# First mixer, two-head units: the first head's turned outputs move from a job's pair of PSUM banks to banks 6 and 7

## What is computed

```python
def ab_mixer(xn, w_in, w_out, lower_bound, a_gnorm, w_gk, b_gk, b_gnorm, s_a, s_b):
    h = jnp.einsum('btd,de->bte', xn, w_in)
    a_q, a_f, a_i, a_g, b_q, b_k, b_v, b_g, b_lr = split_cols(h, AB_SIZES)
    ...
    o_b, s_b_new = gated_linear_recurrence(
        heads(b_q * (B_DK ** -0.5), B_HEADS), heads(b_k, B_HEADS), heads(b_v, B_HEADS),
        heads(log_alpha, B_HEADS), s_b)
    o_b = rmsnorm(o_b, b_gnorm) * jax.nn.silu(heads(b_g, B_HEADS).astype(F32))
    o = jnp.concatenate([o_a.reshape(bsz, t_len, -1), o_b.reshape(bsz, t_len, -1)], axis=-1).astype(xn.dtype)
    return jnp.einsum('bte,ed->btd', o, w_out), s_a_new, s_b_new
```

## Time and profile before

| | us |
|---|---|
| median of 3 runs | 1423.03 |
| lowest, highest run | 1423.01, 1424.56 |
| the profiled execution, its own time | 1427.3 |
| its span, first to last instruction | 1425.5 |
| PE busy in the span | 1391.0 |
| DVE, ACT, POOL busy | 587.2, 558.6, 591.4 |

### The profile page before, as it was taken

How to read it: one execution, slowest core, us unless ns; L and a number is a source line. 1 busy time by engine, 2 the same in 40 slices (tenths; PEclk the granted TensorE clock), 3 DMA queues, 4 the chain that set the end, 5 groups by cost and what they waited for, 6 DMA issues and landing times.

```text
span 1425.5 us, 27289 instructions
## 1 busy us (share of the span) xinstructions
PE 1391.0 (98%) x11038; PEld 1312.6 (92%) x11038; DVE 587.2 (41%) x1068; ACT 558.6 (39%) x907; POOL 591.4 (41%) x303
## 2 busy tenths in 40 slices
PE   8999999999999999999999999999999999999997
PEld 6778898899999999999989778778999999999997
DVE  6615556464321223123425967654633113311234
ACT  5634556445332233122455344444543223321222
POOL 3332222243544344434445466554244433452442
PEclk9999999999999999999999999999999999999999
DMA  5221122242333223322232322111233323332221
GB/s 180 75 74 49 49 77 66 67 130 62 98 85 111 59 88 89 105 73 74 84 103 72 89 76 77 53 31 30 60 89 89 104 74 88 88 104 74 81 68 63
DMA packets 204486, 114.34 MB, mean 80 GB/s; under 512 B 16500, under 2 KB 198648, under 8 KB 204408
## 3 DMA queue, kind: packets, MB, share of 16 engines
q1 hardware_dynamic: 199056, 109.47, 26.4%
q10 hardware_dynamic: 5352, 3.76, 0.8%
HBM read 107.26 MB, written 5.96 MB: 79 GB/s over the span
## 4 chain that ended last, share of the span: by engine, by line
PE 71%; issue 20%; POOL 6%; DVE 1%; ACT 0%; POOLq 0%; DVEq 0%; ACTq 0%
PE ps L1149 57%; POOL w_lo L596 6%; PE ps L1337 3%; PE ps L1284 3%; PE ps L1299 1%; PE ps L1610 1%; PE ps L1654 1%; PE ps L1622 1%; PE ps L1348 0%; PE ps L1646 0%; PE ps L1585 0%; PE ps L1539 0%; DVE small L2205 0%; ACT arena L971 0%; DVE arena L2323 0%
## 5 line engine op out<-in xcount | busy, mean ns | idle before, releaser
L596 POOL TENSOR_TENSOR w_lo<-w_raw,w_hi 128x1024 fp32r<-128x1024 f32 x202 | 501.7, 2487 | 723.5 <-ACT w_hi L661 723.5
L1149 PE MATMUL ps<-x_hi,w_hi 128*128 128x272 f32 (+1 forms) x1840 | 384.7, 290 | 6.2 <-POOL w_lo L596 3.2
L1149 PE MATMUL ps<-x_hi,w_lo 128*128 128x272 f32 (+1 forms) x1840 | 381.6, 289 | 0.0
L1149 PE MATMUL ps<-x_lo,w_hi 128*128 128x272 f32 (+1 forms) x1840 | 380.3, 288 | 0.0
L1149 PEld LDWEIGHTS ps<-x_hi,w_hi 128*128 128x128 f32 (+1 forms) x1840 | 288.9, 188 | 13.5 <-issue 7.0
L1149 PEld LDWEIGHTS ps<-x_lo,w_hi 128*128 128x128 f32 (+1 forms) x1840 | 289.1, 188 | 0.5
L1149 PEld LDWEIGHTS ps<-x_hi,w_lo 128*128 128x128 f32 (+1 forms) x1840 | 287.3, 189 | 0.5
L661 ACT ACTIVATE w_hi<-w_raw 128x1024 fp32r<-128x1024 f32 x202 | 211.4, 1050 | 166.8 <-PE ps L1149 138.6
L1149 PE MATMUL ps<-o_hi,w_hi 128*128 128x272 f32 x832 | 172.4, 288 | 0.2 <-DVE xT L1854 0.2
L1149 PE MATMUL ps<-o_hi,w_lo 128*128 128x272 f32 x832 | 172.2, 288 | 0.0
L1149 PE MATMUL ps<-o_lo,w_hi 128*128 128x272 f32 x832 | 171.5, 288 | 0.0
(11 more groups left out here) (310 smaller groups left out, 1738.0 us busy)
## 6 DMA issues: line engine op xcount, KB each, us to landing
w_raw<-in_ffn_w_in SPq DMA_DIRECT2D x88, 512.0 KB, 3.7
w_raw<-in_ffn_w_out SPq DMA_DIRECT2D x32, 512.0 KB, 3.7
w_raw<-in_ab_w_in SPq DMA_DIRECT2D x28, 512.0 KB, 3.6
w_raw<-in_cd_w_in SPq DMA_DIRECT2D x13, 512.0 KB, 3.6
w_raw<-in_ffn_w_out SPq DMA_DIRECT2D x16, 384.0 KB, 3.4
w_raw<-in_ab_w_out SPq DMA_DIRECT2D x8, 512.0 KB, 4.2
arena<-in_x_prompt SPq DMA_DIRECT2D x4, 512.0 KB, 5.6
w_raw<-in_cd_w_in SPq DMA_DIRECT2D x8, 256.0 KB, 3.4
```

The lines of the kernel that those rows point to most:

```text
L596: pool.tensor_tensor(wl[:, s, :], raw[:, s, :], wh[:, s, :].bitcast(F32), ALU.subtract).then_inc(lo_done, 1)
L1149: mm = pe.matmul(ps[0:M, b + h, 0:HALF], w[:, s, k * M:(k + 1) * M], xs[x][:, k, h * HALF:(h + 1) * HALF], start=(begin and k == ks[0] and ...
```

## The change

The turn of the first head in units 0 and 1 leaves the list of pair users and writes banks 6 and 7, out of which that head's outputs have been read by then. It gets a count of its own, `turn_free`, which `head_gate(u, 0)` raises when it has read the two banks and on which `head_hi(u, 0)`, `head_lo(u, 0)` and the next unit's `turn_and_score` wait. As one entry is gone from the list, the entries behind it move up by one place: the gate job of head 1 takes place 12 (banks 0 and 1), the turn of head 1 place 13 (banks 2 and 3), the score, key and query entries of the next unit the other pair than before, and from the gate job of head 1 of unit 1 on, where two entries are gone, every entry has its old pair again.

```diff
         for e, c0 in enumerate([AG + i * P] if kind == "a" else [BG + 2 * i * P, BG + (2 * i + 1) * P]):
             unit_chunk(c_gates[u], c0)
-            order.append(("turn", u, e))
+            if kind == "a" or e:
+                order.append(("turn", u, e))
...
+        turn_free = sem("turn_free")
+        def turn_bank(u, e):
+            return 2 * (jof["turn", u, e] % 2) if ("turn", u, e) in jof else 6
+        def turn_taken(u, e):
+            return frees(("turn", u, e)) if ("turn", u, e) in jof else turn_free
+        def wait_turn_taken(eng, u, e):
+            if ("turn", u, e) in jof:
+                wait_freed(eng, ("turn", u, e))
+            else:
+                eng.wait_ge(turn_free, units[u][1] + 1)
...
             def head_hi(u, e):
-                wait_freed(act, ("turn", u, e))
+                wait_turn_taken(act, u, e)
...
             def turn_and_score(u):
                 if u > 0:
                     pe.wait_ge(r_r, (NB + 1) * u)
+                    if last(u - 1):
+                        pe.wait_ge(turn_free, units[u - 1][1] + 1)
...
             def turn_outputs(u, e):
-                j = jof["turn", u, e]
                 pe.wait_ge(r_tm, 2 * (heads_before[u] + e + 1))
-                wait_pair(j)
+                if ("turn", u, e) in jof:
+                    wait_pair(jof["turn", u, e])
...
-                    mm = pe.transpose(at(2 * (j % 2), n0, n1), ktm[0:n1 - n0, t, :], ident[0:n1 - n0, 0:n1 - n0])
+                    mm = pe.transpose(at(turn_bank(u, e), n0, n1), ktm[0:n1 - n0, t, :], ident[0:n1 - n0, 0:n1 - n0])
...
             def head_gate(u, e):
-                gn, b0 = pc("ga" if units[u][0] == "a" else "gb"), 2 * (jof[key] % 2)
+                gn, b0 = pc("ga" if units[u][0] == "a" else "gb"), turn_bank(u, e)
...
-                ins.then_inc(frees(key), 1)
+                ins.then_inc(turn_taken(u, e), 1)
...
             def head_lo(u, e):
-                wait_freed(dve, ("turn", u, e))
+                wait_turn_taken(dve, u, e)
```

More of the change, by code:

```diff
@@ L2031, in head_gate @@
             def head_gate(u, e):
-                h, key = heads_before[u] + e, ("turn", u, e)
+                h = heads_before[u] + e
                 dve.wait_ge(r_ot, h + 1)
```

## The result

The changed kernel is slower: a median of 1429.69 us (6 runs, 1426.49 to 1430.66) against 1424.02 us (6 runs, 1423.01 to 1427.25), ratio 1.0037 with a 95% interval of 1.0027 to 1.0048, which is 3.8 to 6.8 us. Taken once more beside other kernels it gave 1429.66 against 1423.66 us, ratio 1.0048 (1.0034 to 1.0062). I had forecast 1423.0 us and no change, with an upper end of 1426.2 us.

The account below looks back on a forecast made before the run. PE, busy 1391.0 of 1425.5 us, was taken as the bound. Removed waits of -2.02 us, +2.02 us given back and 0 for the rest summed to 0 on the median of 1423.03: 1423.0 us, range 1421.0 to 1426.2 us.

Parts of the forecast that it names:

- The wait that goes: Units 0 and 1, PE: second gate job starts right behind the first turn, 1.01 us earlier each, -2.02 us.
- What is late next: Second turn, units 0 and 1: still waits for the normalised second head, so +1.01 us twice is given back, +2.02 us.
- The added wait: Head of the next unit: PE waits for banks 6 and 7's read-out, done 6.7 us before PE gets there; 0 us.
- the new count: First head's high and low part wait for their own count, raised 3.4 us before ACT needs it; 0 us.
- the swapped pairs: Entries that move up: second turn's new pair is released 7.0 us ahead, the others wait for the same predecessors; 0 us.
- The cost that the trace of before doesn't show: PE ahead of the second turn: two idles become one of 1.6 us and the clock may drop; bounds 0 to 3.4 us.
- the last of my signs of being wrong: PE's timeline after the change: a granted clock below 1.00 in the jobs behind would show the forecast wrong.
- The price of a fall: Clock drop behind the second turn in unit 0 or 1: 1.7 us each, from a 3.50 us fall at clock 0.51.
- the clock falls: Longer idle ahead of the second turn drops the clock: one fall 1424.7 us, chance 0.06; two 1426.4 us, chance 0.03.
- The gain kept: ACT and DVE chain shorter unprofiled, second head ready sooner: whole gain gives 1421.0 us; chance 0.08, part or whole.
- the job not moved: Second gate job still begins at 130.88 through something overlooked, so nothing changes: 1423.0 us; chance 0.01.

Follow-up runs that it names:

- e1: Changed kernel with the second gate job again waiting for the first gate job's read-out in both two-head units: 1423.66 us, ratio 1.0002.
- e3: Changed kernel with that wait put back in unit 0 alone, so only unit 1 has the joined idle: 1424.45 us, ratio 1.0005.
- e2: Changed kernel with that wait put back in unit 1 alone, so only unit 0 has the joined idle: 1429.48 us, ratio 1.0040.
- e11: The changed kernel itself, measured once more beside other kernels: 1429.66 us, ratio 1.0048 against the kernel before.
- e4: Changed kernel with 12 matmuls that nobody reads ahead of the second turn in both two-head units: 1423.70 us, ratio 0.9999.
- e7: Changed kernel with 6 matmuls that nobody reads ahead of the second turn in both two-head units: 1423.71 us, ratio 0.9996.
- e6: Kernel before, with the second turn of each two-head unit also waiting for the second gate's sigmoid, lengthening the idle: 1430.92 us, ratio 1.0042.

## Why the prediction was wrong, point by point

- **The wait that goes**: right. The second gate job starts directly behind the turn in both units, and the wait for the read-out is gone.
- **What is late next**: right, and right in size. The second turn waits for the second head, 1.69 and 1.61 us where I had worked out 1.64 and 1.58, at an unchanged 8.40 us from the sigmoid. The gain was given back at once.
- **The added wait, the new count, the swapped pairs at 0**: right. e1 has them all and costs nothing (1.0002).
- **The cost that the trace of before doesn't show, taken at 0**: here the prediction failed, twice over. I had seen that the two idles would become one ahead of small matmuls, set its bounds at 0 and 3.4 us, and chose 0 because the stretch itself had kept the clock with 0.63 us of idle and because 1.57 us of idle at 334.2 had kept it too. But the idle at 334.2 stood between dense jobs; the new one stands ahead of transposes and scores. The two rows I leaned on each had one of the two conditions, and the change joined them. What came is the last of my signs of being wrong, a clock below 1.00 in the jobs behind: e1 to e3 show that the joined idle in unit 0 brings the loss, and at the place itself it is 3.0 to 4.6 us in three profiles. The Trainium skill's page "TensorE: Matmul & The Clock Gate", section "HAM oscillation — how this bites in real kernels", tells of a kernel whose clock was throttled again behind waits for DMA of some 3 to 5 us. The idle here is shorter than those waits, and behind 1.69 us the clock fell in unit 0 all the same, while behind 1.61 us it held in unit 1.
- **The price of a fall, 1.7 us**: too small, and with it the range. I took it from the one fall in the earlier trace rows, 3.50 us long. The fall in unit 0 is 6.8 us long in the changed kernel's profile and 10.1 and 10.3 us in those of e2 and e11 (twice the loss by the clock); timed, it costs 3.0, 4.55 and 4.52 us. The fall at 101 met a dense job almost at once, at 101.74; this one meets 20 scores, which at the lower clock take 4.4 us for 2.59, so that the dense job that follows comes later. This reason is argued from the rows, not tested, and it doesn't tell why e2's fall lasted longer than the changed kernel's, where the scores ended 5.9 to 6.0 us behind the turn in both.
- **The rival "the clock falls"**: the right one, with a chance of 0.06 for one fall and 0.03 for two. I had one fall at 1424.7 us, within the bound of no change. One place alone, unit 0, gave 1429.48 us (e2).
- **The gain kept, the job not moved**: neither happened.

## What to carry to other kernels

Taking a wait away ahead of work whose successor waits for something else only moves the idle; look at where it lands, not only at whether it is given back. Two short idles on the matrix engine can be cheaper than one of the same sum, here when 30 small matmuls followed it (unit 0) and not when 20 did (unit 1); why is not shown. Where an idle can't be used, a few matmuls that nobody reads may keep the clock, as in e4 and e7. And when the granted clock varies between executions, compare medians over many and use a profile only to locate the loss.

## What the runs showed of the hardware

- The granted clock fell behind an idle of 1.69 us followed by transposes and scores (0.57 to 0.66 over 10 to 13 us in the three profiles with the joined idle in unit 0), and held in every profile with 0.63 to 0.92 us at the same place. Behind an idle of 1.61 us with half as many scores it held (unit 1 of the changed kernel, of e3 and of e11), and in one execution of e6 it held behind 1.78 us in unit 0.
- Two executions of one kernel have their falls at different places: of the changed kernel's two profiles the second has one at 919 to 929 us (0.66) that the first has not (1.00 from 919 to 925). The executions of the kernel before lie between 1423 and 1427 us, with mean clocks from 0.997 to 0.993.
- At the lower clock the 20 score matmuls took 4.40 and 4.55 us for 2.59 us, 1.7 to 1.8 times as long; pairs of job matmuls were 0.45 us apart for 0.25.
